# Stick-breaking heads in four interleaved pairs among the tiles of the input projection

## The chip, the cores and the metric

The kernel runs on one core of one Trainium2 chip. The metric is the device time of one execution in microseconds. Three runs of the kernel before took 2008.43, 2011.23 and 2012.39 us; their median is 2011.23 us. All traces are of one execution each, on that one core.

## What is computed

Two transformer blocks in float32 over 512 tokens of width 1024. The change lies in the last one. Its input projection gives eight parts, of which the first four belong to stick-breaking attention (8 heads of 64) and the last four to sliding-window attention (8 heads of 64, 2 key heads):

```python
IN_SPLIT_SIZES = (SB_WIDTH, SB_WIDTH, SB_WIDTH, SB_WIDTH, SW_WIDTH, SW_KV_WIDTH, SW_KV_WIDTH, SW_WIDTH)
proj = h @ w_in[l]
sb_q, sb_k, sb_v, sb_g, sw_q, sw_k, sw_v, sw_g = jnp.split(proj, offsets, axis=-1)
# stick breaking, s < t only
z = jnp.einsum('bqhd,bkhd->bhqk', qb, kb).astype(jnp.float32) * scale
log_beta = jax.nn.log_sigmoid(z)
log_1mb = jnp.where(causal, jax.nn.log_sigmoid(-z), 0.0)
later = lax.cumsum(log_1mb, axis=3, reverse=True) - log_1mb
w = jnp.where(causal, jnp.exp(log_beta + later), 0.0)
y_sb = einsum(w, v) * jax.nn.silu(sb_g)
y_sw = sliding_window_sink_attention(sw_q, sw_k, sw_v, ...) * jax.nn.silu(sw_g)
x = x + gate[:, None, :] * (jnp.concatenate([y_sb, y_sw], axis=-1) @ w_out[l])
return rmsnorm_2(x, final_g)
```

## The kernel before

The order of every engine's work is written out by hand. Engines wait for one another on semaphores, and each engine takes its instructions in the order written.

**Projections.** A weight matrix comes in slabs of 2048 columns (1 MB), loaded on the SyncE queue into one of two `w_raw` buffers. ScalarE writes the high part (`w_hi`, in `split` of its block), VectorE the low part (`w_lo`, L1534). TensorE forms two tiles of 128x512 from a slab in 24 matmuls each (high by high, high by low, low by high, over 8 blocks of the contraction), all through `mm` at L742. VectorE copies each tile out of its PSUM bank and counts `tile_free` up. The input projection `w_in` has 13 slabs and 26 tiles: slabs 0 to 3 are `sb_q` and `sb_k`, 4 and 5 `sb_v`, 6 and 7 `sb_gate`, 8 and 9 `sw_q`, 10 `sw_k` and `sw_v`, 11 and 12 `sw_gate`. The tile for `sw_v` is made of 96 matmuls of 128 columns.

**Stick-breaking heads.** After the last tile the eight heads run one after another. A head has logits by key block j (widths 128, 256, 384 and 512 for j = 3 to 0), in four banks, `bank[4*(h%2)+j]`:

- `logits`: 4 float32 matmuls over 64 rows, head h on rows 0 to 63 or 64 to 127. The trace records a float32 matmul as two.
- `negated_size` on VectorE (L2002, L2003): -|z|, two instructions for each j.
- `softplus_exp` and `softplus_log` on ScalarE (all through `a`, L1227): Exp, then Ln of 1 + that.
- `softplus_sum` on VectorE (L2010, L2011): adds max(z, 0) and masks the diagonal block, two instructions for each j.
- `sticks` on TensorE: 4 bf16 and 10 float32 matmuls that add the masks and the sums over later keys onto the logits in the banks (`not_before`, `minus`, `from_here`).
- Exp of each bank into `sb_w` on ScalarE.
- `stick_values`: 4 float32 matmuls into 64 output rows of bank `4*(h%2)+3`, then the gate on VectorE (L2021), the high part on ScalarE (`h_hi`) and the low part on VectorE (`h_lo`), each of 64 rows.

The logits of head h + 1 are issued ahead of the sticks of head h. `negated_size(h+1)` stands ahead of the gate of head h on VectorE, `softplus_sum(h+1)` behind it.

**After them** come the eight sliding-window heads (TensorE, VectorE and ScalarE by turns: `sw_p` at L2038, `nmax` at L2041), the output projection `w_out` of 4 slabs, the last norm and the transposes out.

Of the kernel before, what the change touches and what calls it, by code (L numbers as in the profile page):

```python
# [38 lines left out]
HD = 64  # L39
# [33 lines left out]


# [52 lines left out]
def build(nc, ins, out):  # L127
# [9 lines left out]
    with ctx:  # L137
# [127 lines left out]
        sp_T = put("softplus", [P, NB, T])  # L265
        sw_T = put("sb_w", [P, NB, T])
        sp_at = here[0]
        wp = put("sw_p", [P, 2, NB, 2 * P])
        wpT = put("sw_pT", [P, NB, 2 * P])
# [3 lines left out]
        from_here = put("from_here", [P, P])  # L273
        ends.append(here[0])
        here[0] = sp_at
        softplus = [sp_T, put("softplus_b", [P, NB, T])]
# [244 lines left out]
        def slab_source(n):  # L521
# [35 lines left out]
            if stage == "w_in":  # L557
                return cols(ins["w_in_2"][0], 256 * s, 256)
# [68 lines left out]
        def _(pool):  # L627
# [107 lines left out]
            pool.wait_ge(tile_free, TILE0["w_in"] + 21)  # L735
# [4 lines left out]
        def _(pe):  # L740
# [338 lines left out]
            for s in range(13):  # L1079
                n = FIRST["w_in"] + s  # L1080
                if s in (4, 5):

                    pe.wait_ge(lo_done, splits_before(n) + 1)
                    wh, wl = view(w_hi[n % 2], DT, 256), view(w_lo[n % 2], DT, 256)
                    for j in range(2):
                        tile = 2 * s + j
                        b = bank[(TILE0["w_in"] + tile) % 4]
                        wait(pe, tile_free, free_before("w_in", tile))
                        for half in range(2):
                            t = 2 * j + half  # L1090
                            for k in range(DT):
                                o, hh, hl = b[:, half * 256:(half + 1) * 256], h_hi[:, k, t * P:(t + 1) * P], h_lo[:, k, t * P:(t + 1) * P]
                                mm(o, hh, wh[:, k, :], k == 0, False)
                                mm(o, hh, wl[:, k, :], False, False)
                                m = mm(o, hl, wh[:, k, :], False, k == DT - 1)
                        m.then_inc(slab_half, 1)
                elif s == 10:

                    pe.wait_ge(lo_done, splits_before(n) + 1)
# [1026 lines left out]
```

## Time and profile before

| What | us |
|---|---|
| Median of three runs | 2011.23 |
| Profiled execution, span from first to last instruction | 2007.5 |
| TensorE busy in the span | 1843.6 (92%) |
| VectorE busy | 1106.5 (55%) |
| ScalarE busy | 687.0 (34%) |
| Second half of the input projection (from its 14th tile copied on) | 1715.8 to 1786.4 |
| Stick-breaking heads | 1787.1 to 1894.2 |
| Sliding-window heads | 1894.2 to 1948.8 |
| Output projection | 1948.8 to 1996.0 |

Each run's time holds what lies around the span as well; the page gives the profiled execution by its span alone, and the median of the runs stands 3.7 us above that. Times in the rows are counted from the span's start. A stage window tells how busy each engine was in it and at what share of full speed TensorE's clock was granted (PEclk, 1.00 is 2.4 GHz and 0.50 is 1.2 GHz). The timeline merges instructions of one kind that follow one another (x8 is eight of them, and the second number runs from the first's start to the last's end). The chain of waits is the work that ended last, followed back.

### The profile page before, as it was taken

How to read it: one execution, taken by the hardware profiler on the slowest of the kernel's cores; microseconds unless marked ns; L12 is line 12 of the kernel's file. 1: busy time of each engine (PE TensorE's matmuls, PEld its weight loads, DVE VectorE, ACT ScalarE, POOL GpSimd, SP SyncE). 2: the span in 40 equal slices, each digit the busy share in tenths (PEclk: the TensorE clock that was granted, in tenths of full speed). 3: DMA queues.
4: the chain of work that ended last, by engine and by line, in shares of the span. 5: the costliest groups of instructions: out<-in, count | busy, mean ns of one | idle time of the engine just before them, and what ended most of it. 6: DMA issues, size and time to landing. Idle time of an engine off the chain costs nothing.

```text
span 2007.5 us, 22255 instructions
## 1 busy us (share of the span) xinstructions
PE 1843.6 (92%) x8470; PEld 1428.0 (71%) x8470; DVE 1106.5 (55%) x1448; ACT 687.0 (34%) x1003; POOL 214.7 (11%) x196
## 2 busy tenths in 40 slices
PE   5988899989999999889899999999999979987788
PEld 4775477778888887555567977788888859864467
DVE  6589754465555324765545544655563473335574
ACT  4221323333333212245433342333331121246562
POOL 1321030110000111133412003000000000000000
PEclk8989999999999999899999999999999989999889
DMA  4244522123233222100112422222223313310001
GB/s 156 84 127 147 167 97 71 47 80 105 84 104 104 94 95 77 33 24 13 63 38 81 135 83 84 78 95 99 85 98 100 102 55 105 101 52 1 0 1 63
DMA packets 156408, 162.12 MB, mean 81 GB/s; under 512 B 2903, under 2 KB 153872, under 8 KB 156336
## 3 DMA queue, kind: packets, MB, share of 16 engines
q1 hardware_dynamic: 155775, 160.44, 24.6%
q8 instruction: 48, 0.79, 0.2%
q0 software_dynamic: 240, 0.53, 0.1%
q14 instruction: 25, 0.20, 0.0%
q10 hardware_dynamic: 320, 0.16, 0.0%
HBM read 158.76 MB, written 2.10 MB: 80 GB/s over the span
## 4 chain that ended last, share of the span: by engine, by line
PE 79%; DVE 11%; issue 4%; ACT 3%; DMA 2%; POOL 1%; DVEq 0%; ACTq 0%; POOLq 0%
PE bank L742 78%; DMA w_raw<-in_w_ada_dram 1%; DVE cv L1617 1%; DVE w_lo L1534 1%; DVE h_lo L1560 1%; ACT sw_p L1227 1%; ACT h_hi L1227 1%; DVE rstd L1552 1%; DVE mla_pT L1937 1%; ACT sb_w L1227 0%; ACT mla_p L1227 0%; PE bank L1046 0%; DVE nmax L1923 0%; DVE sw_p L2038 0%; ACT w_hi L1227 0%
## 5 line engine op out<-in xcount | busy, mean ns | idle before, releaser
L742 PE MATMUL bank<-h_hi,w_hi 128*128 128x512 f32 (+1 forms) x1464 | 581.4, 397 | 45.9 <-DVE h_lo L1534 14.2
L742 PE MATMUL bank<-h_hi,w_lo 128*128 128x512 f32 (+1 forms) x1464 | 573.2, 392 | 0.0
L742 PE MATMUL bank<-h_lo,w_hi 128*128 128x512 f32 (+1 forms) x1464 | 573.1, 391 | 0.0
L1534 DVE TENSOR_TENSOR w_lo<-w_raw,w_hi 128x2048 fp32r<-128x2048 f32 (+2 forms) x144 | 327.2, 2272 | 281.5 <-ACT w_hi L1227 281.0
L1227 ACT ACTIVATE w_hi<-w_raw 128x2048 fp32r<-128x2048 f32 (+2 forms) x144 | 261.0, 1813 | 532.8 <-PE bank L742 527.9
L742 PEld LDWEIGHTS bank<-h_hi,w_hi 128*128 128x128 f32 (+1 forms) x1464 | 276.5, 189 | 123.9 <-issue 38.0
L742 PEld LDWEIGHTS bank<-h_lo,w_hi 128*128 128x128 f32 (+1 forms) x1464 | 277.0, 189 | 57.6 <-issue 1.9
L742 PEld LDWEIGHTS bank<-h_hi,w_lo 128*128 128x128 f32 (+1 forms) x1464 | 276.4, 189 | 58.4
L742 PE MATMUL bank<-g_lo,w_hi 128*128 128x512 f32 x352 | 136.9, 389 | 0.0
L742 PE MATMUL bank<-g_hi,w_lo 128*128 128x512 f32 x352 | 136.9, 389 | 0.0
L742 PE MATMUL bank<-g_hi,w_hi 128*128 128x512 f32 x352 | 136.9, 389 | 0.0
L1227 ACT ACTIVATE fb<-sq,prm 128x512 f32<-128x512 f32 x44 | 35.7, 816 | 162.8 <-DVE sq L1769 162.8
L1617 DVE SCALAR_TENSOR_TENSOR cv<-glu,prm,cv 128x512 f32<-128x512 f32 x120 | 87.4, 798 | 0.0
L1769 DVE TENSOR_TENSOR sq<-bank,rstd 128x512 f32<-128x512 f32 x44 | 30.1, 687 | 92.2 <-PE bank L742 92.0
L742 PEld LDWEIGHTS bank<-g_hi,w_hi 128*128 128x128 f32 x352 | 66.1, 188 | 13.8
L742 PEld LDWEIGHTS bank<-g_lo,w_hi 128*128 128x128 f32 x352 | 66.1, 188 | 13.7
L742 PEld LDWEIGHTS bank<-g_hi,w_lo 128*128 128x128 f32 x352 | 66.1, 188 | 13.6
L679 POOL TENSOR_TENSOR sq<-x 128x512 f32<-128x512 f32 x5 | 5.2, 1040 | 599.0 <-DVE x L1711 329.4
L1711 DVE TENSOR_TENSOR x<-x,bank 128x512 f32<-128x512 f32 x32 | 22.0, 687 | 77.0 <-PE bank L742 76.3
L1227 ACT ACTIVATE g_hi<-fb 128x512 f32 (+1 forms) x44 | 27.7, 632 | 103.6 <-DVE fb L1784 103.6
L681 POOL TENSOR_TENSOR sq<-x 128x512 f32<-128x512 f32 x35 | 38.9, 1112 | 160.7 <-DVE x L1711 88.6
L682 POOL TENSOR_TENSOR sq<-sq,sq 128x512 f32<-128x512 f32 x37 | 55.4, 1498 | 2.9
(313 smaller groups left out, 2511.4 us busy)
## 6 DMA issues: line engine op xcount, KB each, us to landing
w_raw<-in_ffn_w_up_dram SPq DMA_DIRECT2D x44, 1024.0 KB, 5.0
w_raw<-in_xa_wkv_dram SPq DMA_DIRECT2D x16, 1024.0 KB, 5.3
w_raw<-in_ffn_w_down_dram SPq DMA_DIRECT2D x16, 1024.0 KB, 5.2
w_raw<-in_w_in_dram SPq DMA_DIRECT2D x13, 1024.0 KB, 5.2
w_raw<-in_w_ada_dram SPq DMA_DIRECT2D x12, 1024.0 KB, 5.1
w_raw<-in_xa_wq_dram SPq DMA_DIRECT2D x8, 1024.0 KB, 5.1
w_raw<-in_xa_wo_dram SPq DMA_DIRECT2D x8, 1024.0 KB, 5.2
w_raw<-in_pc_w_in_dram SPq DMA_DIRECT2D x6, 1024.0 KB, 5.1
```

The source lines that it names most:

```text
L679: link(nc.gpsimd.tensor_tensor(acc, src(i), src(i), MUL))
L681: link(nc.gpsimd.tensor_tensor(tmp, src(i), src(i), MUL))
L682: m = nc.gpsimd.tensor_tensor(acc, acc, tmp, ADD)
L742: return nc.tensor.matmul(o, w, v, start=start, stop=stop, **kw)
L1227: return nc.scalar.activation(o, i, f, **kw)
L1534: return tt(lo_, v, hi.bitcast(f32), SUB)
L1552: link(nc.vector.reciprocal(r, r))
L1560: stt(lo_[:, i, :], src(i), param(g, o + i), hi[:, i, :].bitcast(f32), MUL, SUB).then_inc(split_lo, 1)
L1617: m = stt(o, src, w, o, MUL, ADD)
L1711: tt(x[:, i, :], x[:, i, :], bank[(TILE0[stage] + i) % 4][:, :], ADD).then_inc(tile_free, 1)
L1769: tt(sq[j][:, :], bank[(tile + j) % 4][:, :], rstd[:, :], MUL).then_inc(tile_free, 1)
L1937: cp(lpT[:, KOFF[j]:KOFF[j] + n], bank[4 + LQ_AT[("T", e, j)] % 3][:, 0:n]).then_inc(lt_done, 1)
```

## The change

1. The slabs of `w_in` come in another order (`W_SLABS`): 0 to 7, then 10, 11, 12, 8, 9. Tiles 0 to 13 run as before. Tiles 12 to 25 use banks 6 and 7 (`w_bank`).
2. The heads run in four pairs. A pair has six banks: three for each head, where j = 2 and j = 3 share one (`stick`). On TensorE a pair is: logits of both heads, alternating by j; two tiles of the projection (`W_BEFORE`); the sticks of the first head, then of the second; one tile (`W_AFTER`); the values of both heads, alternating by j, into rows 0 to 63 of one bank and 64 to 127 of another. Logits for j = 0 wait for the gates of the pair before, since these read the same banks.
3. |z| is one bitwise instruction on VectorE (`size`), and Exp has scale -1. Exp and Ln are loaded as one table at the head of each pair; Silu of the gates stands in pair 0 and pair 2. `sb_w` gets a second buffer.
4. The splits of slabs 8 to 13 stand between the steps of the pairs on ScalarE and VectorE.
5. The gate writes its product back into `sg_T`. The high and low parts of the stick-breaking output are made of 128 rows at once, four times, during the sliding-window heads 1 to 4 (ScalarE) and 2 to 5 (VectorE).

```diff
+W_SLABS = (0, 1, 2, 3, 4, 5, 6, 7, 10, 11, 12, 8, 9)
+W_MEANWHILE = 6
+W_BEFORE = ((14, 15), (17, 18), (20, 21), (23, 24))
+W_AFTER = ((16,), (19,), (22,), (25,))
...
+        def w_bank(i):
+            return bank[6 + i % 2] if i >= 2 * W_MEANWHILE else bank[(TILE0["w_in"] + i) % 4]
+        def stick(h, j):
+            b, c0 = ((0, 0), (1, 0), (2, 0), (2, 2 * P))[j]
+            return bank[3 * (h % 2) + b][:, c0:c0 + (NB - j) * P]
...
+            def w_tile(i):
+                s, j = i // 2, i % 2
+                n, o = FIRST["w_in"] + s, w_bank(i)
+                pe.wait_ge(lo_done, splits_before(n) + 1)
+                if i >= 2 * W_MEANWHILE + 2:
+                    pe.wait_ge(tile_free, TILE0["w_in"] + i - 1)
...
-            def logits(h):
-                wait(pe, so_scaled, h - 1)
-                r0, p = (h % 2) * HD, h // 2
+            def logits(pair):
                 for j in range(NB - 1, -1, -1):
-                    mm(bank[4 * (h % 2) + j][:, 0:(NB - j) * P], sk_T[r0:r0 + HD, p, j * P:(j + 1) * P],
-                       sq_T[r0:r0 + HD, p, j * P:], True, True).then_inc(z_ready, 1)
+                    if j == 0:
+                        wait(pe, so_scaled, 2 * pair)
+                    for h in (2 * pair, 2 * pair + 1):
+                        r0 = (h % 2) * HD
+                        mm(stick(h, j), sk_T[r0:r0 + HD, pair, j * P:(j + 1) * P], sq_T[r0:r0 + HD, pair, j * P:],
+                           j != 2, True, skip_group_check=True).then_inc(z_ready, 1)
...
-            logits(0)
-            for h in range(SBH):
-                if h + 1 < SBH:
-                    logits(h + 1)
-                sticks(h)
-                stick_values(h)
+            def stick_values(pair):
+                pe.wait_ge(w_ready, 8 * pair + 2 * NB)
+                for j in range(NB):
+                    for h in (2 * pair, 2 * pair + 1):
+                        m = mm(stick_out(h)[:, j * P:], sv_N[:, j, h * HD:(h + 1) * HD], sb_w[h % 2][:, j, j * P:],
+                               j == 0, j == NB - 1)
+                        if j == NB - 1:
+                            m.then_inc(so_ready, 1)
+            for pair in range(SBH // 2):
+                logits(pair)
+                for i in W_BEFORE[pair]:
+                    w_tile(i)
+                sticks(2 * pair)
+                sticks(2 * pair + 1)
+                for i in W_AFTER[pair]:
+                    w_tile(i)
+                stick_values(pair)
...
+            for pair in range(SBH // 2):
+                nc.scalar.preload_act_table_set("natural_log_exp_and_others")
+                softplus_log(2 * pair)
+                softplus_log(2 * pair + 1)
+                if pair < 2:
+                    split(n + 8 + 2 * pair)
+                else:
+                    split(n + 7 + 2 * pair)
+                if pair == 0:
+                    gates(sg_T, 6)
+                    nc.scalar.preload_act_table_set("natural_log_exp_and_others")
+                weights(2 * pair)
+                if pair == 0:
+                    split(n + 9)
+                if pair == 2:
+                    split(n + 12)
+                weights(2 * pair + 1)
+                if pair == 2:
+                    gates(wg_T, 9)
...
+                if 1 <= h <= SBH // 2:
+                    act.wait_ge(slab_half, 2 * FIRST["w_out"])
+                    act.wait_ge(so_scaled, SBH)
+                    a(h_hi[:, h - 1, :], sg_T[:, h - 1, :], ACT.Copy).then_inc(so_hi, 1)
...
-                    link(ts(v, z, -1.0, None, MUL))
-                    tt(v, v, z, ALU.min).then_inc(abs_done, 1)
+                    ts(softplus[h % 2][:, j, j * P:].bitcast(i32), stick(h, j).bitcast(i32), 0x7FFFFFFF, None,
+                       ALU.bitwise_and).then_inc(abs_done, 1)
...
+            for pair in range(SBH // 2):
+                first, second = 2 * pair, 2 * pair + 1
+                size(first)
+                size(second)
+                w_out_of(W_BEFORE[pair][0])
+                softplus_sum(first)
+                w_out_of(W_BEFORE[pair][1])
+                softplus_sum(second)
...
+                w_out_of(W_AFTER[pair][0])
+                dve.wait_ge(gate_act, pair + 1)
+                for h in (first, second):
+                    r0 = (h % 2) * HD
+                    dve.wait_ge(so_ready, h + 1)
+                    o = sg_T[r0:r0 + HD, pair, :]
+                    tt(o, stick_out(h), o, MUL).then_inc(so_scaled, 1)
...
+                if 2 <= h <= SBH // 2 + 1:
+                    dve.wait_ge(so_hi, h - 1)
+                    low(h_lo[:, h - 2, :], sg_T[:, h - 2, :], h_hi[:, h - 2, :]).then_inc(so_lo, 1)
```

TensorE before, from the end of head 0's sticks to the logits of head 2:

```order
L742 MATMUL bank<-softplus,from_here 128x512
L742 MATMUL bank<-sb_w,sb_v 64x512
L742 MATMUL bank<-sb_w,sb_v 64x384
L742 MATMUL bank<-sb_w,sb_v 64x256
L742 MATMUL bank<-sb_w,sb_v 64x128
L742 MATMUL bank<-sb_q,sb_k 128x128
L742 MATMUL bank<-sb_q,sb_k 128x256
L742 MATMUL bank<-sb_q,sb_k 128x384
L742 MATMUL bank<-sb_q,sb_k 128x512
```

TensorE in the changed kernel, from the second value matmul of pair 1 (`sb_w_b` is the second head's buffer) to the first matmul of tile 20:

```order
L772 MATMUL bank<-sb_w_b,sb_v 64x512
L772 MATMUL bank<-sb_w,sb_v 64x384
L772 MATMUL bank<-sb_w_b,sb_v 64x384
L772 MATMUL bank<-sb_w,sb_v 64x256
L772 MATMUL bank<-sb_w_b,sb_v 64x256
L772 MATMUL bank<-sb_w,sb_v 64x128
L772 MATMUL bank<-sb_w_b,sb_v 64x128
L772 MATMUL bank<-sb_q,sb_k 128x128 x2
L772 MATMUL bank<-sb_q,sb_k 128x256 x2
L772 MATMUL bank<-sb_q,sb_k 128x384 x2
L772 MATMUL bank<-sb_q,sb_k 128x512 x2
L772 MATMUL bank<-h_hi,w_hi_55 128x512
```

Values and logits now stand head by head in turn, and a tile of the projection (L772 `h_hi,w_hi`) follows the logits where the sticks stood.

ScalarE before, about head 1 (`h_hi` is the high part of head 0's output, 128x128 to 128x512 the four widths of a head):

```order
L1227 ACTIVATE h_hi<-fb_59 64x512
L1227 ACT_TABLE_LOAD
L1227 ACTIVATE softplus<-softplus 128x128
L1227 ACTIVATE softplus<-softplus 128x256
L1227 ACTIVATE softplus<-softplus 128x384
L1227 ACTIVATE softplus<-softplus 128x512
L1227 ACTIVATE sb_w<-bank 128x128
L1227 ACTIVATE sb_w<-bank 128x256
L1227 ACTIVATE sb_w<-bank 128x384
L1227 ACTIVATE sb_w<-bank 128x512
L1227 ACT_TABLE_LOAD
```

ScalarE in the changed kernel, from the head of pair 1 on:

```order
L1512 ACT_TABLE_LOAD
L1261 ACTIVATE softplus<-softplus 128x128
L1261 ACTIVATE softplus<-softplus 128x256
L1261 ACTIVATE softplus<-softplus 128x384
L1261 ACTIVATE softplus<-softplus 128x512
L1261 ACTIVATE softplus<-softplus,ones 128x128
L1261 ACTIVATE softplus<-softplus,ones 128x256
L1261 ACTIVATE softplus<-softplus,ones 128x384
L1261 ACTIVATE softplus<-softplus,ones 128x512
L1261 ACTIVATE softplus_b<-softplus_b 128x128
L1261 ACTIVATE softplus_b<-softplus_b 128x256
L1261 ACTIVATE softplus_b<-softplus_b 128x384
```

The table load between Exp and Ln is gone, and the high part of 64 rows with it; both heads' Exp and Ln stand in one row of work.

VectorE before, from the gate of head 0 (L2021) on:

```order
L2021 TENSOR_TENSOR fb_59<-bank,sb_gate 64x512
L2010 SCALAR_TENSOR_TENSOR softplus_b<-bank,softplus_b 128x128
L2011 TENSOR_TENSOR softplus_b<-softplus_b,before 128x128
L2010 SCALAR_TENSOR_TENSOR softplus_b<-bank,softplus_b 128x256
L2011 TENSOR_TENSOR softplus_b<-softplus_b,before 128x128
L2010 SCALAR_TENSOR_TENSOR softplus_b<-bank,softplus_b 128x384
L2011 TENSOR_TENSOR softplus_b<-softplus_b,before 128x128
L2010 SCALAR_TENSOR_TENSOR softplus_b<-bank,softplus_b 128x512
L2011 TENSOR_TENSOR softplus_b<-softplus_b,before 128x128
L1534 TENSOR_TENSOR h_lo<-fb_59,h_hi 64x512
L2002 TENSOR_SCALAR softplus<-bank 128x128
```

VectorE in the changed kernel, from the gates of pair 0 (L2088) on (L2054 is `size`, L2035 the copy of tile 17 out of its bank):

```order
L2088 TENSOR_TENSOR sb_gate<-bank,sb_gate 64x512 x2
L2054 TENSOR_SCALAR softplus<-bank 128x128
L2054 TENSOR_SCALAR softplus<-bank 128x256
L2054 TENSOR_SCALAR softplus<-bank 128x384
L2054 TENSOR_SCALAR softplus<-bank 128x512
L2054 TENSOR_SCALAR softplus_b<-bank 128x128
L2054 TENSOR_SCALAR softplus_b<-bank 128x256
L2054 TENSOR_SCALAR softplus_b<-bank 128x384
L2054 TENSOR_SCALAR softplus_b<-bank 128x512
L2035 COPY sw_v<-bank 128x512
L2062 SCALAR_TENSOR_TENSOR softplus<-bank,softplus 128x128
```

The sum of a head now stands behind the copy of a tile, and the second instruction of |z| is gone.

## Rows read from the trace of the kernel before

**Rows 1.** stage windows: us, busy us of PE PEld DVE ACT POOL, PEclk, DMA.
```profile
1715.75:1786.40 70.65, 70.60 (x360) 59.91 (x359) 22.61 (x20) 14.96 (x12) 1.13 (x2) 1.00 0.29 93
1787.10:1894.15 107.05, 82.78 (x320) 47.07 (x320) 61.19 (x143) 67.93 (x121) 0.00 (x0) 0.94 0.00 0
1894.15:1948.80 54.65, 39.52 (x218) 30.84 (x218) 42.94 (x98) 34.57 (x112) 0.00 (x0) 0.84 0.00 1
```

**Rows 2.** who waited for whom, 1787 to 1894 us; total, times, longest.
```profile
DVE fb L2021 <- PE bank L742: 40.3, 8, 6.1
...
PE bank L742 <- ACT sb_w L1227: 12.9, 8, 2.2
```

**Rows 3.** VectorE in order of time, input projection; start us, us, then idle before.
```profile
1710.33 0.69 DVE L1982 COPY sb_gate<-bank 128x512 f32<-128x512 f32 x1 [1.17 <-PE bank L742]
1715.77 0.69 DVE L1982 COPY sb_gate<-bank 128x512 f32<-128x512 f32 x1 [4.75 <-PE bank L742]
...
1753.85 0.68 DVE L1986 COPY sw_k<-bank 64x512 f32<-64x512 f32 x1 [1.14 <-PE bank L742]
...
1764.51 0.69 DVE L1989 COPY sw_v<-bank 128x512 f32<-128x512 f32 x1 [9.28 <-PE bank L742]
```

**Rows 4.** TensorE in order of time, stick-breaking heads.
```profile
1787.13 3.19 PE L742 MATMUL bank<-sb_q,sb_k 64*128 64x128 f32 x16 [0.78 <-DVE sw_gate L1991]
...
1830.75 2.42 PE L742 MATMUL bank<-sb_q,sb_k 64*128 64x128 f32 x8 [0.78 <-DVE fb L2021]
1833.11 0.23 PE L742 MATMUL bank<-ident_b,not_before 128*128 128x128 bf16 x1
...
1839.90 2.37 PE L742 MATMUL bank<-sb_w,sb_v 128*64 128x512 f32 x8 [1.84 <-ACT sb_w L1227]
...
1845.41 0.23 PE L742 MATMUL bank<-ident_b,not_before 128*128 128x128 bf16 x1
...
1849.34 1.02 PE L742 MATMUL bank<-softplus,from_here 128*128 128x512 f32 x2
```

**Rows 5.** ScalarE groups by form, 1787 to 1894 us; busy us, mean ns.
```profile
L1227 ACT ACT_TABLE_LOAD x17 | 21.8, 1283 | 0.3
...
L1227 ACT ACTIVATE softplus<-softplus 128x512 f32<-128x512 f32 x4 | 2.5, 629 | 3.2 <-DVE softplus L2003 3.2
```

**Rows 6.** ScalarE in order of time, same stretch.
```profile
1838.45 1.40 ACT L1227 ACTIVATE sb_w<-bank 128x128 f32<-128x128 f32 x4
...
1841.16 1.92 ACT L1227 ACTIVATE softplus<-softplus,ones 128x128 f32<-128x128 f32 x4
```

**Rows 7.** VectorE in order of time, slab split and a head's sum.
```profile
1778.70 2.29 DVE L1534 TENSOR_TENSOR w_lo<-w_raw,w_hi 128x2048 fp32r<-128x2048 f32 x1 [2.50 <-ACT w_hi L1227]
...
1843.03 0.29 DVE L2010 SCALAR_TENSOR_TENSOR softplus<-bank,softplus 128x128 f32<-128x128 f32 x1
...
1845.74 0.29 DVE L2011 TENSOR_TENSOR softplus<-softplus,before 128x128 f32<-128x128 f32 x1
...
1849.16 0.68 DVE L2002 TENSOR_SCALAR softplus_b<-bank 128x512 f32<-128x512 f32 x1
```

**Rows 8.** chain of waits, last gate to first window head; start us, us, what.
```profile
1893.46 0.70 DVE fb L2021
...
1896.09 1.29 DVE sw_p L2038 x4
```

**Rows 9.** chain of waits, one sliding-window head to the next.
```profile
1923.13 1.97 ACT sw_p L1227 x8
1925.29 0.53 ACT h_hi L1227
...
1929.27 1.97 ACT sw_p L1227 x8
```

**Rows 10.** chain of waits, the fifth head's value matmuls; start us, us, what.
```profile
1852.58 4.07 PE bank L742 x8
```

**Rows 11.** a window of the sliding-window stage, columns as in Rows 1.
```profile
1903.00:1911.00 8.00, 7.74 (x28) 6.42 (x29) 5.39 (x12) 4.26 (x16) 0.00 (x0) 0.50 0.01 2
```

More of the change, by code:

```diff
@@ L264, in build @@
         wg_T = put("sw_gate", [P, 4, T])
[L265 to L269, printed above, removed]
         minus = put("minus", [P, P])
@@ L273, in build @@
         from_here = put("from_here", [P, P])
+        softplus = [put("softplus", [P, NB, T])]
+        sb_w = [put("sb_w", [P, NB, T])]
+        sp_at = here[0]
+        wp = put("sw_p", [P, 2, NB, 2 * P])
+        wpT = put("sw_pT", [P, NB, 2 * P])
         ends.append(here[0])
         here[0] = sp_at
-        softplus = [sp_T, put("softplus_b", [P, NB, T])]
+        softplus.append(put("softplus_b", [P, NB, T]))
+        sb_w.append(put("sb_w_b", [P, NB, T]))
+        ends.append(here[0])
         here[0] = arena
@@ L1076, in _ @@
             mm(bank[6][:, :], ones[:, :], sq[1][:, :], True, True).then_inc(stat2_done, 1)
[L1079 to L1099, printed above, removed]
-                    wh, wl = view(w_hi[n % 2], DT, 256), view(w_lo[n % 2], DT, 256)
-                    slab_tile("w_in", n, 20, bank[(TILE0["w_in"] + 20) % 4][:, :], DT,
-                              lambda k: (wh[:, k, 0:P], wl[:, k, 0:P]), h_operand)
-                    b = bank[(TILE0["w_in"] + 21) % 4]
-                    wait(pe, tile_free, free_before("w_in", 21))
@@ L1163, in w_place @@
                 return bank[4 + r % 4]
+            pe.wait_ge(tile_free, TILE0["w_out"])
             pe.wait_ge(so_scaled, SBH)
@@ L1448, in _, with gates, softplus_log @@
                 a(h_hi[:, i, :], fb[i % 2][:, :], ACT.Identity, bias=mod[:, i:i + 1]).then_inc(split_hi, 1)
[L1449 to L1458 removed]
+            n = FIRST["w_in"]
+            for s in range(W_MEANWHILE + 1):
+                split(n + s + 1)
+            def gates(g_T, place):
+                for i in range(4):
+                    act.wait_ge(tile_free, TILE0["w_in"] + 2 * place + i + 1)
+                    a(g_T[:, i, :], g_T[:, i, :], ACT.Silu).then_inc(gate_act, 1)
+            def softplus_log(h):
                 for j in range(NB - 1, -1, -1):
@@ L1994, in _, with size @@
+            n = FIRST["w_in"]
+            for s in range(W_MEANWHILE + 1):
+                if s:
+                    split(n + s + 1)
+                w_out_of(2 * s)
+                w_out_of(2 * s + 1)
             dve.wait_ge(sb_masks, 5)
-            dve.wait_ge(gate_act, 4)
-            def negated_size(h):
+            def size(h):
                 for j in range(NB - 1, -1, -1):
-                    v, z = softplus[h % 2][:, j, j * P:], bank[4 * (h % 2) + j][:, 0:(NB - j) * P]
-                    dve.wait_ge(z_ready, 4 * h + NB - j)
+                    dve.wait_ge(z_ready, stick_step(h, j))
```

156 lines of the change are left out of this document (72 added, 84 removed).

## The prediction

> **What bounds the kernel now.** I read the stage windows first. In the second half of the input projection TensorE is busy 70.60 of 70.65 us at a granted clock of 1.00: this stretch is as long as its matmuls. In the stick-breaking heads no engine is full: TensorE 82.78 us of 107.05, ScalarE 67.93, VectorE 61.19 [rows 1]. A head there takes 107.05 / 8 = 13.4 us. The waits say what it is made of: TensorE waits 12.9 us in eight waits for the Exp of the last bank, and VectorE waits 40.3 us for the values before it can apply the gate [rows 2]. So the heads are bound by a ring from TensorE to VectorE to ScalarE and back, with the next head only partly beside it, and the projection by TensorE alone. What the change can win is TensorE's idle time in the ring, plus whatever its matmuls gain by standing in another order.
>
> **The work of TensorE, by rows.** A tile: 1715.77 - 1710.33 = 5.44 us. The tile of `sw_v`, 96 short matmuls: 1764.51 - 1753.85 = 10.66 us [rows 3]. Logits of one head alone 2.42 us; its values 2.37 us; its sticks from 1845.41 to 1849.34 + 1.02 = 4.95 us [rows 4], of which some 0.15 us is the tail of the last matmul, which overlaps what follows: 4.8 us.
>
> Two heads in turn are a term of their own. At the start of the stage the logits of heads 0 and 1 stand one behind the other and take 3.19 us together, where one head alone takes 2.42 us [rows 4]. The second head adds 0.77 us, not 2.4: its matmuls, on rows 64 to 127 of the array, run beside those of rows 0 to 63. Written in turn, equal widths lie side by side, so I take 2.42 us for a pair; the ends are 2.42 and, with no overlap at all, 4.84 us. For the values the trace has no such pair: two heads in turn differ by output rows (0 to 63, 64 to 127) and not by contraction rows. The ends are 2.37 us (side by side) and 4.74 us (one behind the other). I take 2.45 us, since the nearest row, the pair of logits, shows halves of the array working at once.
>
> The Trainium skill, "TensorE: Matmul & The Clock Gate", section on row/col tiling, states the same gain for small output rows as for small contraction rows; by it the term is the lower end, as I took it, and no run here shows it yet. The same skill, "TensorEngine Tiling (Array Packing)", Key Properties, says that changing the tiling mode drains TensorE, which speaks against this change with four changes of shape in a pair. The row: logits over 64 rows end at 1830.75 + 2.42 = 1833.17 and the first stick matmul over 128 rows is recorded from 1833.11 [rows 4]. So the trace shows no more than the usual tail. By the rule as a full wait for the last result, I would add about 0.15 us for each of 16 changes, 2.4 us; by the row, 0.
>
> **The sum.** Old stretch, from the 14th tile's copy at 1715.77 to the end of the last gate at 1893.46 + 0.70 = 1894.16 [rows 3, 8]: 178.4 us. New, if TensorE never waits for the chains:
>
> - 11 tiles x 5.44 = 59.8, and `sw_v` 10.7: 70.5
> - logits 4 x 2.42 = 9.7
> - sticks 8 x 4.8 = 38.4
> - values 4 x 2.45 = 9.8
> - gates: logits of j = 0 wait for two gates of 0.70 us [rows 8] and 0.1 us of signal. The logits of the other three widths (768 of 1280 columns, 60% of 2.42 = 1.45 us) run meanwhile: 0.1 us left, I take 0.3 for each pair: 1.2
> - hand-overs at 16 places, 0.1 us each: 1.6 (my choice; the ends are 0 and 0.3 each)
> - the last pair's gates, with nothing beside them: 1.5
>
> 132.7 us, so 45.7 us less.
>
> **Whether the chains hide.** I laid one pair out from the end of the values before it (0.0). VectorE's gates end at 1.5. Logits of j = 0 end at 2.8. `size` is one instruction where there were two, 0.68 us for 512 columns [rows 7]; for four widths about 1.9 us a head, so both heads are through at 5.4. ScalarE: Ln of a head takes 1.92 us [rows 6], Exp about as much (0.629 us for its widest [rows 5]); four such rows of work from 3.5, where the first head's widest arrives, end at 9.8 for the second head. A table load costs 1.283 us, and there were 17 in the stage [rows 5]; now one at each pair's head, which ScalarE runs while it waits for logits, and four more around the gates' Silu in pairs 0 and 2. TensorE is in its first tile until 8.2 and in the second until 13.7. VectorE must copy the first tile before it sums the first head: 8.9 + 3.0 (a head's sum, 1845.74 + 0.29 - 1843.03 [rows 7]) = 11.9, 1.8 us ahead of the sticks. It copies the second at 13.7 and sums the second head from 14.4 to 17.4; its sticks begin at 18.5. The weights' Exp (1.40 us a head [rows 6]) follow the sticks and end at 23.9, under the third tile, which ends at 28.8. Values end at 31.2. The splits of slabs (2.29 us on VectorE [rows 7]) fall behind the second sum and under the third tile; what waits behind them on VectorE is only the copy of that tile. In pair 0 ScalarE also has two table loads, four gates and a second split: some 7 us between 14 and 21, under the sticks and the third tile. So every chain has cover, the tightest by 1.8 us. If one lost it, each us over would cost 1 us, in up to four pairs. The slab loads on SyncE come at each split, at least a pair ahead of the tile that needs them, where before they came every 11 us; the copy of `sw_k` across partitions on GpSimd comes earlier too. Nothing there is on the path.
>
> **The sliding-window heads.** At their start the high and low part of the last stick head go: from the gate's end at 1894.16 to the first `sw_p` at 1896.09 there are 1.9 us [rows 8], of which a memset and the signal stay: 1.3 us less. Then each of four rounds gets a high part of 128x512 on ScalarE and a low part on VectorE. The chain runs through exactly this place: Exp of a head, then `h_hi` 0.53 us, then the rest, 1929.27 - 1923.13 = 6.14 us a head [rows 9]. ScalarE's added copy stands in it, about 0.65 us in three rounds, 0.2 in the first, and VectorE's last one, in the shadow of the Exp, 0.4: 2.6 us more. Ends: 0 (all in shadow) and 4 x 1.3 = 5.2.
>
> **Total.** -45.7 - 1.3 + 2.6 = -44.4 us. Durations are from the profiled execution, whose span is 2007.5 us, 3.7 us under the median run; the page gives no other time for it, so I carry the difference over to the median: 2011.2 - 44.4 = 1966.8, 1967 us.
>
> **The rivals.**
>
> *The values of a pair do not run side by side.* Nothing in the trace shows output halves at once; for it speaks only the likeness to logits. 4 x 2.3 = 9.2 us more: 1976 us. Chance 0.17.
>
> *A chain comes late.* The cover of the first sum is 1.8 us, and VectorE takes its work in order, so a late copy or sum holds up the sticks. If the whole sum of the second head (3.0 us) stood open in each pair: 12 us more, 1979 us. Against it: the sticks need only the narrowest block first. Chance 0.11.
>
> *Slower: the clock.* The chain shows eight value records of the fifth head at 4.07 us against 2.37 us for the same eight [rows 10, 4], and a window of the sliding-window heads at 0.50, the lower level of 1.2 GHz [rows 11]. Both come after waits of TensorE. If the pairs, with their 64-row shapes and short waits, were granted 0.50 for more than 44 of their 131 us, the gain would be gone; at 0.50 for two thirds of the stretch the time is 1967 + 87 = 2054 us. Against it: the stick stage with far longer waits still had 0.94 on average [rows 1]. Chance 0.03.
>
> *The change does not do what it says*: the tables are switched all the same, or the waits on the copies of tiles make a ring as slow as before. The order of ScalarE shows no load between Exp and Ln, so this would be the ring: about 2011 us. Chance 0.02.
>
> *More than forecast.* TensorE waits less before the sliding-window heads and keeps 1.00 where it had 0.84 [rows 1]; an 8 us window at 0.50 [rows 11] given back is 4 us, and with hand-overs at 0 and the added copies in shadow 4 more: 1959 us. Chance 0.05.
>
> **How the numbers follow.** The forecast has 0.62 and a range of its own of 1962 to 1972 us (hand-overs, added copies, one window of the clock either way). The range of 8 in 10 takes in the values one behind the other and the better case: 1957 to 1978 us. A time within 0.2% of the one before (about 4 us, what a measurement of this kernel can tell from no change) has 0.02, slower 0.03, faster 0.95.
>
> **What would show it.** In the profile after: the 14th tile's copy still at about 1716 us; the last gate of L2088 at about 1848; TensorE over 95% busy between them at a clock near 1.00; 16 logit records in about 2.4 us and 16 value records in about 2.4 (4.7 is the first rival); waits of TensorE for the sums of `softplus` near 0 (over 2 us a pair is the second); the sliding-window heads some 1 to 3 us longer than 54.65 us. I am wrong if the stretch from the 14th copy to the last gate is over 145 us, or if the clock in it is under 0.9.

## The result, and the profile after

| | Kernel before | Changed kernel |
|---|---|---|
| Median, us | 2011.81 (4 runs, 2008.43 to 2017.44) | 1964.62 (4 runs, 1960.12 to 1967.84) |
| Ratio, 95% interval | 1 | 0.9769 (0.9749 to 0.9789) |
| Span of the profiled execution | 2007.5 | 1965.8 (its own time 1967.84) |
| 14th tile's copy to the end of the last gate | 178.4 | 131.1 |
| From there to the value matmuls of the last sliding-window head, by the chain of waits | 54.7 | 56.0 |
| From the last gate to the end of the span | 113.3 | 113.2 |

The change makes the kernel 47 us faster; 44.4 were forecast. The profiled execution starts the 14th copy at 1721.51 us, 5.7 us later than the one before. The code ahead of it is the same, and it started between 1713.2 and 1721.5 in all thirteen traces of this document, so that part is scatter. The stretch is 47.3 us shorter and what follows it 0.2; less the 5.7 us of the later start, that is the 41.7 us by which the two spans differ (to the rounding).

The stage windows of the changed kernel, columns as in [rows 1]: the new stretch, the sliding-window heads, and what follows them up to 1955 us.

```profile
1721.50:1852.60 131.10, 129.44 (x680) 95.38 (x680) 64.47 (x124) 63.52 (x116) 1.13 (x2) 1.00 0.16 51
1852.60:1908.60 56.00, 41.37 (x219) 32.62 (x219) 44.74 (x101) 35.92 (x115) 0.00 (x0) 0.82 0.00 1
1908.60:1955.00 46.40, 45.49 (x207) 37.44 (x207) 23.75 (x28) 11.04 (x12) 0.00 (x0) 1.00 0.07 23
```

The first row answers to the first two of [rows 1] together. There TensorE was busy 70.60 + 82.78 = 153.4 of 178.4 us and idle 25.0. Now it is busy 129.4 and idle 1.7. So of the 47.3 us, 23.3 are waits of TensorE that are gone, and 23.9 are less time busy for the same matmuls. The clock is 1.00 throughout. VectorE (64 of 131 us) and ScalarE (64) are now half idle beside it.

Where did 23.9 us of busy time go? Part of it is clock. Four stretches of the old heads read 0.50 on the same view of the kernel before:

```profile
1795.00:1798.40 3.40, 3.28 (x13) 2.58 (x12) 3.26 (x10) 2.14 (x4) 0.00 (x0) 0.50 0.00 0
1853.00:1856.40 3.40, 3.40 (x8) 1.36 (x6) 0.00 (x0) 2.74 (x5) 0.00 (x0) 0.50 0.00 0
1859.80:1863.20 3.40, 3.40 (x14) 2.88 (x14) 3.26 (x10) 0.73 (x2) 0.00 (x0) 0.50 0.00 0
1880.30:1883.70 3.40, 3.40 (x8) 1.23 (x6) 0.00 (x0) 2.61 (x5) 0.00 (x0) 0.50 0.00 0
```

13.6 us at the lower level are 6.8 us lost. The rest is the array used by halves: the values of eight heads were 8 x 2.37 us and are four pairs of 2.37, and the logits were 3.19 for the first two and 6 x 2.42, and are 4 x 2.43 by their work: 9.5 + 8.0 us. With the clock's 6.8 that is 24.3, against 23.9 read.

TensorE in order of time, the last value matmuls of pair 0 and what follows (`sb_w` is the first head's, `sb_w_b` the second's):

```profile
1751.94 0.27 PE L772 MATMUL bank<-sb_w,sb_v 128*64 128x128 f32 x1
1751.94 0.27 PE L772 MATMUL bank<-sb_w_b,sb_v 128*64 128x128 f32 x1
...
1752.26 2.76 PE L772 MATMUL bank<-sb_q,sb_k 64*128 64x128 f32 x16
1754.95 0.33 PE L772 MATMUL bank<-w_hi,h_hi 128*128 128x128 f32 x1
```

The two heads' matmuls start within 0.01 us of each other and run side by side. The last pair shows it in full, from its first record to the end of its last:

```profile
1848.76 0.64 PE L772 MATMUL bank<-sb_w,sb_v 128*64 128x512 f32 x1
1848.77 0.64 PE L772 MATMUL bank<-sb_w_b,sb_v 128*64 128x512 f32 x1
...
1850.86 0.27 PE L772 MATMUL bank<-sb_w_b,sb_v 128*64 128x128 f32 x1
...
1852.74 2.52 PE L772 MATMUL bank<-sw_k,sw_q 64*128 64x128 f32 x16 [1.61 <-issue]
```

1850.86 + 0.27 - 1848.76 = 2.37 us for sixteen records, what one head's eight took in [rows 4]. The 1.61 us ahead of the sliding-window heads are TensorE's wait for the last two gates.

The chain of waits through the stretch (start us, us, what) is TensorE with one gate at each pair's start:

```profile
1719.89 32.49 PE bank L772 x159
1752.52 0.62 issue
1753.14 0.71 DVE sb_gate L2088
1753.89 34.96 PE bank L772 x212
```

And the waits by engine and line, 1721.5 to 1852.6 us (total, times, longest), the two that answer to [rows 2] and the one that is new:

```profile
ACT softplus L1261 <- DVE softplus L2054: 29.8, 8, 8.9
...
DVE sb_gate L2088 <- PE bank L772: 6.0, 4, 1.7
...
PEld bank L772 <- DVE sb_gate L2088: 2.0, 3, 0.7
```

VectorE's 40.3 us of waiting for the values are now 6.0. ScalarE waits 29.8 us for |z|, which costs nothing here. TensorE's 12.9 us of waiting for `sb_w` have no row left; what remains is its wait for the gates.

### The profile page after: what moved, and what is told of

Read it like the earlier page. It is cut to its first block, busy times and chain, and to the rows that moved or that the text cites. A ratio compares the mean times of both kernels' runs of the same rounds, so it can differ in the third digit from the quotient of the medians.

```text
span 1965.8 us, 22201 instructions
## 1 busy us (share of the span) xinstructions
PE 1829.0 (93%) x8470; PEld 1423.1 (72%) x8470; DVE 1088.9 (55%) x1412; ACT 668.7 (34%) x988; POOL 214.9 (11%) x196
## 4 chain that ended last, share of the span: by engine, by line
PE 81%; DVE 10%; issue 4%; ACT 2%; DMA 2%; POOL 1%; DVEq 0%; POOLq 0%; ACTq 0%
PE bank L772 80%; DMA w_raw<-in_w_ada_dram 1%; DVE cv L1665 1%; DVE w_lo L1582 1%; DVE h_lo L1608 1%; DVE rstd L1600 1%; ACT h_hi L1261 1%; DVE mla_pT L1985 1%; ACT sw_p L1261 0%; ACT mla_p L1261 0%; DVE nmax L1971 0%; PE bank L1076 0%; ACT w_hi L1261 0%; DVE nmax L2104 0%; DVE sw_p L2101 0%
## 5 line engine op out<-in xcount | busy, mean ns | idle before, releaser
L772 PE MATMUL bank<-h_hi,w_hi 128*128 128x512 f32 (+1 forms) x1464 | 586.2, 400 | 46.1 <-DVE h_lo L1582 14.7
L772 PE MATMUL bank<-h_hi,w_lo 128*128 128x512 f32 (+1 forms) x1464 | 575.5, 393 | 0.0
L772 PE MATMUL bank<-h_lo,w_hi 128*128 128x512 f32 (+1 forms) x1464 | 575.4, 393 | 0.0
L772 PEld LDWEIGHTS bank<-h_hi,w_hi 128*128 128x128 f32 (+1 forms) x1464 | 277.9, 190 | 127.4 <-issue 41.1
L772 PEld LDWEIGHTS bank<-h_lo,w_hi 128*128 128x128 f32 (+1 forms) x1464 | 278.6, 190 | 58.7 <-issue 2.9
L772 PEld LDWEIGHTS bank<-h_hi,w_lo 128*128 128x128 f32 (+1 forms) x1464 | 277.8, 190 | 59.5
L772 PE MATMUL bank<-g_hi,w_hi 128*128 128x512 f32 x352 | 136.9, 389 | 0.0
L772 PE MATMUL bank<-g_lo,w_hi 128*128 128x512 f32 x352 | 136.9, 389 | 0.0
L772 PE MATMUL bank<-g_hi,w_lo 128*128 128x512 f32 x352 | 136.9, 389 | 0.0
L772 PEld LDWEIGHTS bank<-g_lo,w_hi 128*128 128x128 f32 x352 | 66.1, 188 | 13.8
L772 PEld LDWEIGHTS bank<-g_hi,w_hi 128*128 128x128 f32 x352 | 66.1, 188 | 13.7
L772 PEld LDWEIGHTS bank<-g_hi,w_lo 128*128 128x128 f32 x352 | 66.1, 188 | 13.7
```

What stands on the lines that cost most here:

```text
L772: return nc.tensor.matmul(o, w, v, start=start, stop=stop, **kw)
```

## The experiments

Each kernel below was timed beside runs of the kernel before; ratios are to those. "Stretch" is read as in the table: start of the 14th copy to the end of the last gate, and it repeats far better than the whole: 131.13 and 131.09 us in two executions of the changed kernel whose spans are 1965.8 and 1960.4.

### Heads of a pair one behind the other

**Values.** `values_apart` turns the two loops of `stick_values`:

```diff
-                for j in range(NB):
-                    for h in (2 * pair, 2 * pair + 1):
+                for h in (2 * pair, 2 * pair + 1):
+                    for j in range(NB):
```

> The changed kernel with the value matmuls of a pair head by head instead of in turn (same matmuls, same waits). Theory: the two heads' values run side by side on two halves of the output columns, 2.4 us a pair; head by head only the narrowest block of the first lies beside the widest of the second, so a pair takes about 4.3 us, 1.9 us more, 7 to 9 us in all: the stretch from the 14th tile's copy to the last gate goes from 131.1 to about 139 us, the time from 1964.6 to about 1972. Rival: order does not matter, TensorE's gain is all from the tiles between: 0 +- 2 us.

Measured: 1970.51 us, 0.9805 (0.9769 to 0.9841); stretch 135.53 us, 4.4 longer. TensorE at the end of its pair 0:

```profile
1748.02 1.93 PE L772 MATMUL bank<-sb_w,sb_v 128*64 128x512 f32 x5
1749.58 0.64 PE L772 MATMUL bank<-sb_w_b,sb_v 128*64 128x512 f32 x1
...
1750.49 1.46 PE L772 MATMUL bank<-sb_w_b,sb_v 128*64 128x384 f32 x6
1751.88 2.00 PE L772 MATMUL bank<-sb_q,sb_k 64*128 64x128 f32 x14
```

The direction fits, the size doesn't (7 to 9 us by the theory, 0 +- 2 by the rival): the theory let only the first head's narrowest block lie beside the second head's widest, 4.3 us a pair. In the trace the second head's first record already starts with the first head's block of 256 columns (1749.58 us in pair 0), as neighbours overlapped in [rows 4]. The values take 1751.88 - 1748.02 = 3.86 us to the start of the next logits where the changed kernel takes 2.31, so 6.2 us more in four pairs. And the first head's gate is done earlier: the logits of pair 2 take 2.43 us and not 2.76, 1.0 us in three pairs, and the wait for the last gates is 0.83 us and not 1.61. 6.2 - 1.0 - 0.8 = 4.4, as read. These two are, in order of time in this run:

```profile
1789.55 2.43 PE L772 MATMUL bank<-sb_q,sb_k 64*128 64x128 f32 x16
...
1855.22 2.52 PE L772 MATMUL bank<-sw_k,sw_q 64*128 64x128 f32 x16 [0.83 <-issue]
```

**Logits.** `logits_apart` does the same to the logits (and to the counts that VectorE waits for):

```diff
-                for j in range(NB - 1, -1, -1):
-                    if j == 0:
-                        wait(pe, so_scaled, 2 * pair)
-                    for h in (2 * pair, 2 * pair + 1):
+                for h in (2 * pair, 2 * pair + 1):
+                    for j in range(NB - 1, -1, -1):
+                        if j == 0:
+                            wait(pe, so_scaled, 2 * pair)
```

> The changed kernel with the logits of a pair head by head. Theory: as heads 0 and 1 did in the kernel before (3.19 us for both), so 0.8 us more a pair than in turn, and up to 0.6 us more of waiting for the gates, since the first head's widest block now comes earlier: 3 to 5 us in all, the stretch 131.1 to about 135. Rival: logits hidden or equal: 0 +- 2 us.

Measured: 1970.86 us, 0.9798 (0.9761 to 0.9834); stretch 135.78 us, 4.65 longer. Its logits of pair 1 against the row at 1752.26 above:

```profile
1752.60 4.06 PE L772 MATMUL bank<-sb_q,sb_k 64*128 64x128 f32 x16
```

That is 1.3 us more in a pair that begins behind gates. In the first pair, which waits for no gate, the logits take 3.19 us in this run as well, 0.8 more. 3 x 1.3 + 0.8 = 4.7, as read. The first head's widest matmul now stands early and runs into the gate's wait, with only three narrower ones ahead of it. The theory of 3 to 5 us holds. The order inside a pair is worth some 4.5 us for each of the two steps and not twice that, since neighbours in series overlap in part anyway: of the 2.4 us that two heads can share, the logits in series still share 1.65 (4.84 - 3.19) and the values 0.8 (4.74 - 3.93, to the end of the last record).

### What the pairs and the tiles are worth apart

`tiles_first` puts all 26 tiles, and with them the splits and the gates' Silu, ahead of the pairs, as before, and leaves the pairs as they are. TensorE's part of it:

```diff
-            for i in range(2 * W_MEANWHILE + 2):
+            for i in range(26):
                 w_tile(i)
...
                 logits(pair)
-                for i in W_BEFORE[pair]:
-                    w_tile(i)
                 sticks(2 * pair)
                 sticks(2 * pair + 1)
-                for i in W_AFTER[pair]:
-                    w_tile(i)
                 stick_values(pair)
```

> The changed kernel with all 26 tiles of the projection ahead of the pairs and none between them; splits and gates of the projection stand ahead too. Pairs, one table and one-instruction |z| stay. Theory: a pair then shows its ring: logits 2.4, size, Exp, Ln and the first sum until about 7.7 us, sticks to about 17.5, Exp 0.7, values 2.4, gates 1.5: about 21 to 22 us a pair against 14.8 us of its share with tiles between, so 25 to 29 us slower than the changed kernel (about 1992), and still some 20 us faster than before. Rival (all of the gain is tiles in idle time): the time of before, 2011. Second rival (the gain is the shorter ring and the halves, tiles between give little): within 8 us of the changed kernel.

Measured: 1986.48 us, 0.9899 (0.9853 to 0.9944); stretch 156.14 us. Its two stage windows and the waits of TensorE in the second:

```profile
1714.00:1786.90 72.90, 72.90 (x376) 61.20 (x374) 24.57 (x23) 19.26 (x19) 1.13 (x2) 1.00 0.28 91
1786.90:1870.10 83.20, 64.20 (x306) 39.88 (x304) 40.30 (x101) 43.27 (x97) 0.00 (x0) 0.90 0.00 1
```

```profile
PE bank L772 <- DVE softplus L2051: 14.6, 4, 3.7
PE bank L772 <- ACT sb_w_b L1257: 2.7, 4, 0.7
```

So of 47.3 us, the tiles between the steps bring 156.1 - 131.1 = 25.0 and all the rest of the change 22.3. The 25.0 can be read off: without tiles TensorE waits 14.6 us for the first sums and 2.7 us for `sb_w_b` (17.3), and it is busy 72.90 + 64.20 = 137.1 us where the changed kernel is 129.4 (7.7), at a clock of 0.90 for the pairs. The matmuls are the same; the stretches of the pairs at 0.50 cost some 8 us of their time (an estimate from windows of 0.4 us), so those 7.7 us are the clock. The theory's 25 to 29 us holds at its lower end by the stretch; the medians, of few runs each, lie 21.9 us apart. Neither rival holds: the stretch is 22.3 us below that of before and 25.0 above that of the changed kernel.

The 22.3 us can be read off in part as well. Against the kernel before, TensorE is busy 16.3 us less (137.1 against 153.4) and idle 6.0 us less (19.0 against 25.0). The halves in turn take 17.5 us off the busy time, as above, and a lower clock puts some 1.4 back (8.1 against 6.7 us lost to 0.50).

### |z| and the table, in either kernel

In the kernel before, each edit alone:

```diff
# before_one_table
+            nc.scalar.preload_act_table_set("natural_log_exp_and_others")
             softplus_exp(0)
# before_abs
-                    link(ts(v, z, -1.0, None, MUL))
-                    tt(v, v, z, ALU.min).then_inc(abs_done, 1)
+                    ts(v.bitcast(i32), z.bitcast(i32), 0x7FFFFFFF, None, ALU.bitwise_and).then_inc(abs_done, 1)
...
-                    a(v, v, ACT.Exp).then_inc(exp_done, 1)
+                    a(v, v, ACT.Exp, scale=-1.0).then_inc(exp_done, 1)
```

> The kernel before with one table for Exp and Ln in the stick-breaking heads, 16 loads of 1.28 us fewer. Theory: most loads lay beside TensorE or VectorE; on the chain is the one between Exp and Ln of head 0 (2 loads, 2.6 us) and little more: 2 to 5 us faster than before. Rival: the loads are in every head's ring: 8 x 1.3 = 10 us or more faster.

> The kernel before with |z| in one bitwise instruction on VectorE instead of two. Theory: the two instructions of the widest blocks stand in the chain of every head (VectorE busy 61 of 107 us), about 1.9 us of VectorE a head saved of which 0.7 to 1.2 us is on the chain: 6 to 10 us faster than before. Rival: hidden beside TensorE's sticks: 0 +- 2 us.

Measured: `before_one_table` 2005.65 us, 0.9991 (0.9976 to 1.0005), stretch 175.18, 3.2 shorter; `before_abs` 2003.83 us, 0.9965 (0.9952 to 0.9979), stretch 168.22, 10.2 shorter. By the stretch the first theory (2 to 5 us) holds and the second (6 to 10) is met at its upper end. The heads of the first, then of the second:

```profile
1784.50:1888.30 103.80, 82.00 (x320) 47.28 (x320) 61.22 (x143) 46.77 (x105) 0.00 (x0) 0.93 0.00 0
```

```profile
1790.70:1887.60 96.90, 81.28 (x320) 47.13 (x320) 45.87 (x111) 68.67 (x121) 0.00 (x0) 0.95 0.00 1
```

The first edit lowers ScalarE's busy time by 21 us (67.93 to 46.77) and the stage by 3. The second lowers VectorE's by 15 (61.19 to 45.87) and the stage by 10. In the ring of [rows 2] ScalarE switched its tables mostly while it had nothing to do, and VectorE's |z| stood on the ring. By the medians, the first edit alone can't be told from no change.

In the changed kernel, each taken back: `tables_back` drops both loads of the common table, and `both_back` also restores the two instructions of |z|:

```diff
# tables_back
-                nc.scalar.preload_act_table_set("natural_log_exp_and_others")
                 softplus_log(2 * pair)
...
                     gates(sg_T, 6)
-                    nc.scalar.preload_act_table_set("natural_log_exp_and_others")
# both_back, besides
-                    a(v, v, ACT.Exp, scale=-1.0).then_inc(exp_done, 1)
+                    a(v, v, ACT.Exp).then_inc(exp_done, 1)
...
-                    ts(softplus[h % 2][:, j, j * P:].bitcast(i32), stick(h, j).bitcast(i32), 0x7FFFFFFF, None,
-                       ALU.bitwise_and).then_inc(abs_done, 1)
+                    v, z = softplus[h % 2][:, j, j * P:], stick(h, j)
+                    link(ts(v, z, -1.0, None, MUL))
+                    tt(v, v, z, ALU.min).then_inc(abs_done, 1)
```

> The changed kernel with Exp and Ln from two tables again, 13 loads of 1.28 us more on ScalarE (16.7 us). Theory: ScalarE has cover under the tiles (the first head's Ln ends about 1.3 us later, still before its sum, which waits for a tile's copy; the second's 3.9 us later, about 0.6 us before its sum): 0 +- 2 us. Rival: the missing loads are part of the gain: 5 to 16 us slower than the changed kernel.

> The changed kernel with Exp and Ln from two tables and |z| in two instructions on VectorE, as before (16.7 us more on ScalarE, about 15 us more on VectorE in the pairs). Theory: both lie under the tiles: VectorE is through with |z| at about 7.3 us of a pair instead of 5.4, the second head's Ln ends at about 15.8, its sum at 17 to 18, its sticks begin at 18.5: the stretch stays at 131 us, +- 2. Rival: the cover is used up and each pair shows 2 to 4 us: the stretch at 139 to 147 us.

Measured: `tables_back` 1966.6 us, 0.9784 (0.9749 to 0.9819), stretch 131.14; `both_back` 1962.82 us, 0.9771 (0.9757 to 0.9786), stretch 131.17. The stretch of the one and of the other:

```profile
1719.80:1850.90 131.10, 129.43 (x680) 95.36 (x680) 64.50 (x124) 80.86 (x129) 1.13 (x2) 1.00 0.16 51
```

```profile
1718.00:1849.10 131.10, 129.45 (x680) 95.40 (x680) 79.35 (x156) 80.47 (x129) 1.13 (x2) 1.00 0.16 51
```

17 us more of ScalarE and 15 us more of VectorE cost nothing: the tiles cover both. Part 3 of the change, worth some 13 us where the heads form a ring if its two gains add up, is worth 0.0 once the tiles stand between. Both theories hold.

### A tile kept for later

The new stretch is as long as TensorE's matmuls, and the stage behind it has 56.0 - 41.4 = 14.6 us of idle TensorE and a clock of 0.82. `tile_later` moves the last tile there, behind the scores of the second sliding-window head, where TensorE waits for the softmax (the last two lines are VectorE's copy of it):

```diff
-W_AFTER = ((16,), (19,), (22,), (25,))
+W_AFTER = ((16,), (19,), (22,), ())
...
+            if i == 25:
+                return bank[1]
...
+                if h == 1:
+                    w_tile(25)
...
+                if h == 2:
+                    w_out_of(25)
```

> The changed kernel with the last tile of the projection (sw_q of heads 6 and 7) taken out of the last pair and put behind the logits of sliding-window head 1, where TensorE was idle for 5.9 us; it goes to bank 1 and VectorE copies it ahead of head 2. Theory: 5.4 us less in the last pair, about 1 us given back since the values now wait for the Exp of the weights, the tile hides in the idle time, and TensorE may keep 2.4 GHz there (up to 4 us more): 4 to 8 us faster than the changed kernel, about 1958. Rival: the sliding-window chain is held up by the tile or by its copy: 0 +- 2 us.

> The version with the last tile behind the logits of sliding-window head 1 once more, beside the changed kernel. Theory: its trace showed 4.1 us less from the 14th tile's copy to the end, so 3 to 5 us faster than the changed kernel in these rounds. Rival: the 4.1 us were the clock's granting in one execution: within 1.5 us.

> The changed kernel once more, to compare the two versions below with it in one set of rounds: 1964 +- 3 us by every theory.

Measured: `tile_later` 1961.87 us, 0.9763 (0.9745 to 0.9781). In a later set of runs, all on one chip, `tile_later_again` 1959.7 us, 0.9759 (0.9745 to 0.9772), and the changed kernel itself, `after_again`, 1962.45 us, 0.9775 (0.9762 to 0.9789). The stretch is 126.4 us, 4.7 less: a tile of 5.44 that is gone, less 0.69 for a wait that it had covered. TensorE in `tile_later_again`:

```profile
1842.79 0.64 PE L774 MATMUL bank<-sb_w,sb_v 128*64 128x512 f32 x1 [0.69 <-ACT sb_w_b L1267]
...
1846.77 3.70 PE L774 MATMUL bank<-sw_k,sw_q 64*128 64x128 f32 x16 [1.61 <-issue]
1850.40 0.79 PE L774 MATMUL bank<-h_hi,w_hi 128*128 128x512 f32 x1
1850.99 0.63 PE L774 MATMUL bank<-h_lo,w_hi 128*128 128x512 f32 x1
...
1858.04 0.93 PE L1239 MATMUL bank<-ident,sw_p 128*128 128x128 f32 x7
```

The sliding-window heads of this kernel and of `after_again`:

```profile
1846.70:1902.00 55.30, 43.21 (x241) 33.30 (x242) 43.85 (x99) 35.81 (x115) 0.00 (x0) 0.91 0.00 1
```

```profile
1847.10:1902.50 55.40, 41.73 (x218) 32.85 (x218) 43.94 (x98) 35.90 (x115) 0.00 (x0) 0.82 0.00 1
```

The 24 matmuls of the tile lengthen this stage by 0.5 us (58.3 against 57.8 to the first matmul of `w_out`). They run at half clock at first (0.63 us against 0.39 for the same matmul), so the tile takes until 1858.04 and the transposes behind it come 2.8 us later, counted from the last gate, than in `after_again`. The higher clock behind them pays most of that back: the score matmuls after the transposes take 1.78 us where those of `after_again` take 3.35. From the 14th copy to the end of the span it is 240.2 us in both traces with the later tile, against 244.3 and 244.4 in both of the changed kernel: 4.1 and 4.2 us won, within the theories' 4 to 8 and 3 to 5. The medians of the shared set differ by 2.7 us, less than the theory asked for and with overlapping ranges, so the gain stands on the traces more than on the timing.

`tile_later_halves` moves, beside that, the high parts of the stick-breaking output to other places among ScalarE's work of two heads:

```diff
-                if 1 <= h <= SBH // 2:
+                if h in (1, 2):
...
-                    a(h_hi[:, h - 1, :], sg_T[:, h - 1, :], ACT.Copy).then_inc(so_hi, 1)
+                    k = 0 if h == 1 else 3
+                    a(h_hi[:, k, :], sg_T[:, k, :], ACT.Copy).then_inc(so_hi, 1)
...
+                    if h == 1:
+                        for k in (1, 2):
+                            a(h_hi[:, k, :], sg_T[:, k, :], ACT.Copy).then_inc(so_hi, 1)
```

> The same, with the high parts of the second and third 128 rows of the stick-breaking output made after the scaling of head 1, where ScalarE waited 1.7 us, instead of in the rounds of heads 2 and 3. Theory: each stood in the chain of its round with 0.6 us: 1 to 1.5 us faster than the version above. Rival: the rounds have other work of the same length: 0 +- 0.5 us in the trace.

Measured: 1958.6 us, 0.9763 (0.9748 to 0.9777); 239.8 us from the 14th copy on, 0.4 less than `tile_later_again`. That is within the rival's half microsecond and not what the theory asked for. It is the lowest median of the study, and can't be told from `tile_later_again`.

## Why the prediction was right

The time (1964.62 us, forecast 1967) lies in the forecast's own range of 1962 to 1972, and for the reason given: the new stretch is as long as TensorE's matmuls, 131.1 us where the sum had 132.7. What stands behind the stretch, where 1.3 us more were forecast, is 0.2 us shorter. Both misses are small and go the same way; the sliding-window part below was right in part by luck.

Its terms can be read off one pair. TensorE in order of time: the logits of pair 0, which wait for no gate, then pair 2 step by step (each "..." leaves out the rest of a step):

```profile
1721.41 2.43 PE L772 MATMUL bank<-sb_q,sb_k 64*128 64x128 f32 x16
...
1788.73 2.76 PE L772 MATMUL bank<-sb_q,sb_k 64*128 64x128 f32 x16
1791.42 0.50 PE L772 MATMUL bank<-h_hi,w_hi 128*128 128x512 f32 x1
...
1802.44 0.23 PE L772 MATMUL bank<-ident_b,not_before 128*128 128x128 bf16 x1
...
1807.23 0.22 PE L772 MATMUL bank<-ident_b,not_before 128*128 128x128 bf16 x1
...
1811.15 1.02 PE L772 MATMUL bank<-softplus_b,from_here 128*128 128x512 f32 x2
1811.61 0.79 PE L772 MATMUL bank<-h_hi,w_hi 128*128 128x512 f32 x1
...
1817.59 0.64 PE L772 MATMUL bank<-sb_w,sb_v 128*64 128x512 f32 x1
...
1819.90 2.76 PE L772 MATMUL bank<-sb_q,sb_k 64*128 64x128 f32 x16
```

| Step, start to start | Forecast | Read |
|---|---|---|
| Logits and the wait for gates | 2.42 + 0.3 | 2.69 |
| Two tiles | 10.88 | 11.02 |
| Sticks of both heads and a tile | 9.6 + 5.44 | 15.15 |
| Values | 2.45 | 2.31 |
| Hand-overs | 0.4 | in the rows above |
| Pair | 31.5 | 31.2 |

- **Values.** The choice between 2.37 and 4.74 was the largest open one, and the nearest row had pointed the right way. The first rival, that output halves never run at once, is refuted by the records at 1848.76 and 1848.77. Even heads in series take 3.9 us and not 4.74, and the run with that order cost 4.4 us, not the 9.2 of no overlap at all. The Trainium skill, "TensorE: Matmul & The Clock Gate", "Part 3: Packing small matmuls — row/col tiling", holds that small outputs in different column groups overlap as small contractions do. The traces agree: 2.37 us for the values of two heads, 2.43 for their logits.
- **Gates.** 2.76 - 2.43 = 0.33 us in three pairs, 1.0 in all where the sum had 1.2 for four.
- **Sticks.** 1807.23 - 1802.44 = 4.79 against 4.8. The tile behind the second head's starts inside the last stick matmul's tail.
- **Hand-overs** were mis-sized: 0.14 us in the two tiles and 0.11 in the sticks and the third, 0.25 a pair where 0.4 was put. The Trainium skill, "TensorEngine Tiling (Array Packing)", "Key Properties", has the rule that a change of tiling mode drains TensorE; the prediction's estimate by it was 2.4 us, 0.6 a pair. The trace does not agree with an addition of that size. A pair has three changes of shape (into the logits, out of them, into the values) and not the four of the prediction, and all hand-overs together add 0.25 us to the lengths of the pieces. What a change shows is some 0.1 us between two starts, 0.32 us from the last tile record to the first value record (1817.59) where tile records stand 0.23 apart. Most of that was already in the pieces, which were measured to the end of their last record.
- **The chains hide.** The first sum of pair 2, VectorE in order of time, against the sticks at 1802.44:

```profile
1800.62 0.29 DVE L2063 TENSOR_TENSOR softplus<-softplus,before 128x128 f32<-128x128 f32 x1
```

The margin is 1.5 us where 1.8 had been laid out. The prediction called this the tightest cover, but its own layout had less for the second head, 17.4 against 18.5 us. That sum ends 1.0 us ahead of its sticks at 1807.23:

```profile
1805.94 0.29 DVE L2063 TENSOR_TENSOR softplus_b<-softplus_b,before 128x128 f32<-128x128 f32 x1
```

Neither came late. `both_back` shows that the covers are larger than these rows alone suggest, since 15 us more on VectorE were free: |z| lies ahead of the copy of the tile, which waits for TensorE in any case (3.4 us in pair 2).

- **The clock, 0.03.** It was 1.00 in the whole stretch, with no sign of the rival. The old heads' stretches at 0.50 needed no term of their own: the tiles' and sticks' durations came from rows at full clock, so the 6.8 us of the old stage at 0.50 were in the 178.4 and not in the new terms.
- **The sliding-window heads, +1.3 net** (-1.3 and +2.6). By the chain of waits 54.7 us before and 56.0 after, +1.3, but both terms are off by some 0.7 and cancel, which is luck. The start saves 0.6 us and not 1.3. From the last gate to the first maximum (`nmax`) it is 3.25 us before and 2.68 after:

```profile
1897.40 1.23 DVE nmax L2041
...
1855.32 1.23 DVE nmax L2104
```

The high and low part at this place had hidden the first score matmuls; with them gone VectorE waits 0.61 us for TensorE. The rounds behind it cost 1.8 us and not 2.6. ScalarE's added high part does stand on the chain, beside the old one of [rows 9]:

```profile
1877.40 0.52 ACT h_hi L1261
1877.94 0.64 ACT h_hi L1261
```

Counted to the first matmul of `w_out` the stage comes out even (57.8 and 57.6), because the last value matmuls take 3.15 us at a clock of 0.50 before and 1.64 at 1.00 after. The sum had no term for that; the forecast's range had allowed for some clock either way.

That the sum was right does not mean that each part was worth what it seemed. The prediction never split its 45.7 us by part of the change, and the experiments do: 25.0 for the tiles, 22.3 for the rest, of which |z| and the table are worth something only without the tiles. What |z| and the tables bring inside the 22.3 was not measured in `tiles_first`; the 10.2 and 3.2 us are of the kernel before.

## What to carry to other kernels

Put the matmuls of an independent stage between the steps of a chain, then price the stage as TensorE's work alone and check each chain against the tiles that cover it. Where the cover holds, edits of the other engines' work are worth nothing, as the 17 and 15 us here. Where small matmuls use half of the rows or half of the output rows, write the two halves in turn. Read a stage's waits before shortening an engine in it: 21 us less of ScalarE won 3 in the ring, and 15 us less of VectorE won 10.

## What the runs showed of the hardware beyond what was expected

- Matmuls with 64 output rows in different halves run together as fully as those with 64 contraction rows: sixteen float32 records in 2.37 us, the time of eight.
- The same wait, another clock: after the last gates' 1.61 us, sixteen score records took 3.70 us in `tile_later_again`, the first of them at half clock, and 2.52 in the changed kernel. Both had read 1.00 over the whole stretch ahead. All three traces with the later tile have the slow form (3.70 to 3.75 us), both of the changed kernel the fast one. What differs in the rows ahead is the missing tile and a further wait of 0.69 us four microseconds earlier; what decides was not tried.
- Two executions of one and the same code before the 14th copy can differ by more than the last experiments' effects (1715.96 to 1721.51 us for the changed kernel), while its stretch repeats to 0.04 us. For small effects the stage is the better measure than the total.
